# fp32 matmuls of probabilities with values and of side input with its weight, each as two of 64 stationary columns

## What is computed

```python
probs = jax.nn.softmax(logits, axis=-1)
return jnp.einsum('bqhn,bqnd->bqhd', probs, v_sel)           # attention: 16 heads of 128, 256 keys
...
ff = hier_moe(h, ...)
ple = (p[l] @ w_ple[l]) * jax.nn.sigmoid(h @ w_ple_gate[l])  # p: 256 x 256, w_ple: 256 x 2048
h = layer_norm(DN_ALPHA * h + ff + ple, ln2_g[l], ln2_b[l])
```

## Time and profile before

| | us |
|---|---|
| median of 3 runs | 1674.72 (1673.94 to 1682.01) |
| span of the profiled execution | 1676.2 |
| TensorE matmul busy | 1631.4 |
| VectorE busy | 1154.6 |
| ScalarE busy | 912.3 |
| 24 matmul records of L615, busy | 11.6 |
| 32 matmul records of L730, busy | 15.8 |

### The profile page before, as it was taken

How to read it: one execution, slowest core, us unless ns; L and a number is a source line. 1 busy time by engine, 2 the same in 40 slices (tenths; PEclk the granted TensorE clock), 3 DMA queues, 4 the chain that set the end, 5 groups by cost and what they waited for, 6 DMA issues and landing times.

```text
span 1676.2 us, 21239 instructions
## 1 busy us (share of the span) xinstructions
PE 1631.4 (97%) x7472; PEld 1335.1 (80%) x7472; DVE 1154.6 (69%) x1298; ACT 912.3 (54%) x1066; POOL 103.4 (6%) x84
## 2 busy tenths in 40 slices
PE   8999999999999999999999889999999999999993
PEld 6887888888778888888888578887888888888872
DVE  5546765567465554544465687588899989889897
ACT  4444444545444444444443454577778777777772
POOL 0000000253000000000000140000010000001001
PEclk9999999999999999999999999999999999999997
DMA  8654556453435565556586326499999989999992
GB/s 281 199 175 151 176 176 199 153 175 127 151 126 176 176 201 190 188 199 197 181 324 209 104 99 202 166 406 375 322 350 375 375 292 371 364 329 343 365 371 84
DMA packets 153420, 394.83 MB, mean 236 GB/s; under 512 B 12928, under 2 KB 15616, under 8 KB 135936
## 3 DMA queue, kind: packets, MB, share of 16 engines
q1 hardware_dynamic: 144768, 384.46, 65.1%
q10 hardware_dynamic: 8576, 9.36, 1.6%
HBM read 391.69 MB, written 2.10 MB: 235 GB/s over the span
## 4 chain that ended last, share of the span: by engine, by line
PE 83%; DMA 7%; DVE 6%; ACT 2%; issue 1%; SPq 0%; POOL 0%; DVEq 0%; ACTq 0%
PE bank L435 25%; PE bank L440 25%; PE bank L436 25%; DMA w_ring<-in_w_gate_dram 2%; DVE w_lo L1350 2%; DMA w_ring<-in_w_up_dram 2%; DMA w_ring<-in_w_down_dram 2%; PE bank L824 2%; ACT w_hi L949 1%; PE bank L462 1%; PE bank L593 1%; PE bank L615 1%; DMA w_ring<-in_w_in_dram 1%; PE bank L527 1%; DVE res L1738 0%
## 5 line engine op out<-in xcount | busy, mean ns | idle before, releaser
L1350 DVE TENSOR_TENSOR w_lo<-w_ring,w_hi 128x1024 fp32r<-128x1024 f32 x728 | 877.5, 1225 | 398.2 <-ACT w_hi L949 387.9
L949 ACT ACTIVATE w_hi<-w_ring 128x1024 fp32r<-128x1024 f32 x728 | 760.0, 1055 | 476.3 <-PE bank L440 414.7
L435 PE MATMUL bank<-w_hi,xT_hi 128*128 128x512 f32 (+1 forms) x864 | 347.4, 402 | 2.4 <-ACT w_hi L949 2.4
L436 PE MATMUL bank<-w_hi,xT_lo 128*128 128x512 f32 (+1 forms) x864 | 335.7, 389 | 0.0
L440 PE MATMUL bank<-w_lo,xT_hi 128*128 128x512 f32 (+1 forms) x864 | 229.3, 387 | 0.0
L435 PE MATMUL bank<-w_hi,xg_hi 128*128 128x512 f32 x512 | 200.8, 392 | 0.0
L436 PE MATMUL bank<-w_hi,xg_lo 128*128 128x512 f32 x512 | 199.4, 389 | 0.0
L435 PEld LDWEIGHTS bank<-w_hi,xT_hi 128*128 128x128 f32 x864 | 162.9, 189 | 38.9 <-issue 7.2
L436 PEld LDWEIGHTS bank<-w_hi,xT_lo 128*128 128x128 f32 x864 | 163.1, 189 | 32.5 <-issue 1.9
L440 PEld LDWEIGHTS bank<-w_lo,xT_hi 128*128 128x128 f32 x864 | 161.7, 188 | 33.3
L440 PE MATMUL bank<-w_lo,xg_hi 128*128 128x512 f32 x512 | 158.2, 390 | 0.8 <-DVE w_lo L1350 0.6
(11 more groups left out here) (295 smaller groups left out, 1664.5 us busy)
## 6 DMA issues: line engine op xcount, KB each, us to landing
w_ring<-in_w_in_dram SPq DMA_DIRECT2D x104, 1024.0 KB, 5.0
w_ring<-in_w_gate_dram SPq DMA_DIRECT2D x64, 1024.0 KB, 5.1
w_ring<-in_w_up_dram SPq DMA_DIRECT2D x64, 1024.0 KB, 5.6
w_ring<-in_w_down_dram SPq DMA_DIRECT2D x64, 1024.0 KB, 6.9
w_ring<-in_w_proj_a_dram SPq DMA_DIRECT2D x16, 1024.0 KB, 5.0
w_ring<-in_w_proj_m_dram SPq DMA_DIRECT2D x16, 1024.0 KB, 5.0
w_ring<-in_w_out_dram SPq DMA_DIRECT2D x16, 1024.0 KB, 5.0
w_ring<-in_w_ple_gate_dram SPq DMA_DIRECT2D x16, 1024.0 KB, 4.9
```

The costliest lines, as they stand in the source:

```text
L435: mm(b, lh(k, m), WH[:, s, kk, 0:width], start=start and kk == 0, stop=False)
L436: mm(b, ll(k, m), WH[:, s, kk, 0:width], start=False, stop=False)
L949: fn(WH[:, h % 4, :, 0:width], W32[:, h // 2, 2 * (h % 2):2 * (h % 2) + 2, 0:width], ACT.Copy).then_inc(hi_ready, 1)
L1350: v.tensor_tensor(WL[:, h % 4, :, 0:width], W32[:, h // 2, 2 * (h % 2):2 * (h % 2) + 2, 0:width], WH[:, h % 4, :, 0:width].bitcast(F32), A ...
```

## The change

Every matmul of `values` and of `ple_product` is issued as two. The first has stationary columns 0 to 63 and writes partitions 0 to 63 of the bank, the second has columns 64 to 127 and writes partitions 64 to 127. The moving operand is the same for both. The loop over the contraction is outside, the one over the halves inside; the increment hangs on the last matmul.

```diff
                 for st in range(u // 4 + 1):
-                    last = mm(B[4 + u % 2][:, :], V[:, st, :], PT[:, st, (u % 2) * NC:(u % 2) * NC + NC],
-                              start=st == 0, stop=st == u // 4)
+                    for c in range(2):
+                        last = mm(B[4 + u % 2][64 * c:64 * c + 64, :], V[:, st, 64 * c:64 * c + 64],
+                                  PT[:, st, (u % 2) * NC:(u % 2) * NC + NC], start=st == 0, stop=st == u // 4)
                 last.then_inc(pv_mm, 1)
...
                 for k in range(2):
-                    last = mm(B[6 + n % 2][:, :], pT[:, k, a * P:a * P + P], wple[:, k, c * NC:c * NC + NC],
-                              start=k == 0, stop=k == 1)
+                    for r in range(2):
+                        last = mm(B[6 + n % 2][64 * r:64 * r + 64, :], pT[:, k, a * P + 64 * r:a * P + 64 * r + 64],
+                                  wple[:, k, c * NC:c * NC + NC], start=k == 0, stop=k == 1)
                 last.then_inc(pp_mm, 1)
```

## The result

| | before | after |
|---|---|---|
| median of 7 runs | 1674.7 us | 1689.0 us |
| lowest to highest | 1673.2 to 1682.0 | 1680.4 to 1699.6 |
| profiled execution | span 1676.2 | 1688.3, span 1686.6 |
| records of matmuls on PE | 7472 | 7528 |

The ratio is 1.0088, with an interval of 1.0066 to 1.0111: 14.7 us slower (11 to 19). By the bound of 0.5% this is slower, to which the prediction gave 0.25. The forecast of 1678.4 was 10.6 us too low. The time lies in the range, but only because the range had been stretched for another case.

A forecast was written before the change was run, and what follows sets the result against it. The prediction took TensorE (PE), busy for 97% of the span, to bound the kernel. Adding 3.3 us for values and 0.4 us for side products to 1674.7 gave 1678.4 us, with a range of 1673 to 1697.

The forecast's parts named there:

- Side by side: Both split products: the two halves stream together, 0.857 us per product as before, plus switching costs; chance 0.63.
- Staircase: Rival: passes start strictly in issue order, so each step has one pass more; 1682.7 us, chance 0.08.
- one after the other: Rival: column halves cannot stream at once, so every product takes four passes; 1696.7 us, chance 0.20.
- in turn without a switch: Rival: halves run as narrow matmuls of the full array, in turn, with no mode switch; 1693 us, chance 0.05.
- the quicker pass: Rival: 64 stationary columns halve a pass in values and side products; 1671.6 us, chance 0.04.
- The mode price: Entering and leaving half-array mode on PE: 0.41 us a visit, 3.3 us for eight values steps in attention.
- L558's 0: The other bound for entering half-array mode: a transpose with 8 stationary columns that showed no added time.
- The side products: Side input times its weight, three visits: two covered by PE waits of 0.63 and 3.66 us, the last costing 0.4.
- Product 7: Last side-input product, on the path: 0.4 us, perhaps 0.8 at half clock; a full clock would give back 1.6.
- The sum for what it covered: Values steps 3.3 us plus side-input products 0.4 us: 3.7 us over the median of before, 1678.4 us.
- part (1): Both split products: passes double, nothing else is touched, leaving only whether halves run together and what the mode costs PE.
- the rival of four passes in turn: Both split products: halves run serially, four passes per product; 1696.7 us, chance 0.20, setting the range's upper end.

The follow-up runs named there:

- one_half: The changed kernel issuing only the first half of each split product, so half of these outputs is missing; one run, 1677.7 us.
- halves_outside: The changed kernel with the loops exchanged in the values product: all passes of the first half before any of the second; one run, 1679.0 us.
- after_mm64: The changed kernel with 16 small fp32 matmuls (64 instructions) added at the head of TensorE's program; 1679.4 us, ratio 1.0038 to before.
- values_only: The kernel before with only the products of probabilities with values split (48 added instructions); 1680.5 us, ratio 1.0026.
- mm112: The kernel before with 28 small fp32 matmuls (112 instructions) at the head of TensorE's program, no column tiles; 1689.2 us, ratio 1.0094.
- cut112: The kernel before with 56 output-projection matmuls each cut into two of 256 moving columns (112 more instructions), no column tiles; 1687.9 us, ratio 1.0072.
- after_pad32: The changed kernel with 32 empty instructions that never reached the program, so a repeat of after; 1686.6 us, profiled execution 1678.4 us.
- mm144: The kernel before with 36 small fp32 matmuls (144 instructions) at the head of TensorE's program; 1686.0 us, ratio 1.0064.

## Why the prediction was right and wrong

**Side by side: right.** Starts come in pairs, the first run of L732 takes 10.52 us for 48 records against 10.46 for 24, and the second half is free by `one_half`. Staircase, one after the other, and in turn without a switch are refuted, and so is the quicker pass: a half of 64 columns still takes about 0.43 us a pass, as the length of that run shows.

**The mode price: right, a little high.** 0.41 us was taken from L527; 0.34 is measured at a values step, and 2.75 us for the eight against 3.3. The fall is on the side of L527's 0.41 and not of L558's 0, so the choice of the nearest row was right.

**The side products: right.** The cover of 0.63 us before the first turn absorbed part of the entry (0.50 is left), that of 3.66 is 3.52 now, and the stretch costs 0.1 to 0.2 us instead of 0.4. Product 7 ran at half clock again (3.29 us). What the switch of mode added there and what the clock took or gave can't be told apart in one execution.

**The sum for what it covered: right.** The two fastest executions of the changed program took 1678.4 (profiled, no stall) and 1680.4 us, `halves_outside` without a stall 1679.0, and `after_mm64` 1679.4 with 0.5 us of extra work at its head. Forecast: 1678.4. The ratio of `values_only` gives 4.4 us (2.5 to 6.4), and its trace 2.7, which lies within. That of `after_mm64` gives 6.4 us (4.0 to 8.9), and its trace 2.9 + 0.5: here at least 0.6 us have no row.

**The step that failed** is part (1): "So there are two questions only". There was a third. I counted the added instructions (24 passes to 48, 32 to 64), and asked what each costs where it runs. I didn't ask what 112 more of them do to the code behind them. The missing term is 8.5 to 9.2 us for each stall at the loop's two returns: a branch of 4.2 to 5.9 us, PE idle for 6.2 to 6.3 us, then 2 to 3 us lost at half clock. With none to two in an execution, the median got about one, and 1678.4 + 9 = 1687.4 is near to the 1689.0 measured. The rows to ask for stood in the trace of before: the branches of PE's sequencer at the end of each round (226, 215 and 83 ns), and the instruction queue, silent for 310 us while PE runs through the loop's second and third rounds. A silent queue says that the code in use is held. What looks like the price of a jump to code that isn't held stood there too, in the last branch of PE's kernel code, which skips the unused overflow round:

```profile
L926 PEldq COMPARE_BRANCH  x1: 3378/3378/3378, 1649.7 to 1649.7; - x1
```

A packet of instructions was fetched at 1650.7, 1 us behind its start, and the branch takes 3.4 to 4.9 us in every kernel here. Held code is a resource, like a buffer, and the change moved what had to fit.

The Trainium skill (Runtime: NRT & Kernel Launch, Instruction fetch mechanics) has the mechanism: a taken branch whose target is not in the fetched window forces a fetch before execution goes on. The traces agree, with 4.2 to 5.9 us for the branch. The page gives PE room for 2048 instructions in blocks of 256. One round of this loop has 1560 instructions on PE (records between two returns) and so touches seven or eight such blocks, depending on where it begins; an estimate from the page's figures is that with the block that is fetched ahead it fits in one case and not in the other. That eight are touched just with 112 more fits the table, but no run reads which block is held. The eight packets that after fetched behind its stall agree with a whole body fetched again. The same section also says that only two blocks are held. The quiet queue of before, 310 us with two returns, speaks against this for PE.

**What stays open.** Why the same program stalls in one execution and not in the next, and which block is missing, isn't shown. In after a packet was fetched at 1244.1, 0.7 us before the branch at 1244.8; in `mm112` and `cut112` one came within 2 us behind it; in `after_pad32`, which didn't stall, the last was at 1220.3. This looks like a race between the fetch ahead and the branch. `mm144` fetched one at 1250.1, 0.4 us before its branch at 1250.5, and had no stall; its body may touch one block fewer than with 112, but that isn't shown. So only the dependence on the count of instructions is shown, not the rule by which it decides.

**The range** held the time through the rival of four passes in turn, which is false. The 1697 us of that case happen to be about those of two stalls. That the range held is luck, and 0.73 for no change was too sure: each case I had listed was about the tiles, and none about the rest of the program.

## What to carry to other kernels

A tile of 128 stationary columns cut into two of 64 gains nothing in fp32: the halves do run together, but together they take the time of the whole, plus 0.34 us for each visit between full-width matmuls. Where a kernel has a loop that the hardware runs, count the instructions of its body and those that an edit adds anywhere ahead of it, and look at the loop's returns and at the instruction queue in the trace. Here the 112 instructions, added between 337 and 965 us, cost three times as much for each stall at the loop's return as where they run. When a program's times fall into steps rather than spread, profile a short execution and a long one of it: two traces of the same code show what a comparison with another kernel can't.

## What the runs showed of the hardware

- Column halves seem to have an order each: in `halves_outside` two passes began 14 ns apart, and if the second was the other half's, as the 0.48 us between passes in `one_half` imply, it overtook three passes that stood before it in the program.
- A return of the loop on PE took 0.22 to 0.24 us where no instructions were fetched behind it, and 4.2 to 5.9 us where a round's worth was. PE's idle time is longer than the branch (6.3 us against 4.3 in after), and half clock follows.
- A small fp32 matmul (8 moving columns, 128 stationary) took 0.213 us a pass at the head of the program, at half clock. The same line's weight loads have records of 285 to 338 ns, so I take it that they and not the 8 columns set the pace; that wasn't tried.
- Empty instructions at the head of PE's program left no trace in the program that ran. To move code, instructions that do something are needed.
